# Sliding-window attention: 20 projection units in place of 24, and a new order of dense and attention work

## The reference, cut to what matters

```python
def swa_sink_mixer(h, cos, sin, w_in, sinks, w_out):
    q, k, v, gate = jnp.split(
        h @ w_in, [ATT_WIDTH, ATT_WIDTH + ATT_KV_WIDTH, ATT_WIDTH + 2 * ATT_KV_WIDTH], axis=-1)
    q = apply_partial_rope(q.reshape(b, L, ATT_Q_HEADS, D).astype(f32), cos, sin)
    k = apply_partial_rope(k.reshape(b, L, Hk, D).astype(f32), cos, sin)
    ...
    s = jnp.einsum('bnikgd,bnjkd->bnkgij', qb, kb) * (D ** -0.5)
    ...
    s = jnp.where(valid[None, :, None, None], s, -jnp.inf)
    sink = sinks.astype(f32).reshape(Hk, ATT_GQA)[None, None, :, :, None, None]
    m = jnp.maximum(jnp.max(s, axis=-1, keepdims=True), sink)
    p = jnp.exp(s - m)
    denom = jnp.sum(p, axis=-1, keepdims=True) + jnp.exp(sink - m)
    o = jnp.einsum('bnkgij,bnjkd->bnikgd', p / denom, vb)
    o = o.reshape(b, L, ATT_WIDTH) * jax.nn.silu(gate.astype(f32))
    return o.astype(h.dtype) @ w_out
```

## Time and profile before

| | |
|---|---|
| median of 3 runs | 2375.59 us (2370.33 to 2377.56) |
| the profiled execution: its own time | 2370.34 us |
| its span | 2368.2 us |
| PE busy | 2182.2 us, 92% |
| VectorE busy | 1474.7 us, 62% |
| ScalarE busy | 1020.0 us, 43% |
| SWA from its first rotations to its last P·V | 541.46 to 753.36 us |

### The profile page before, as it was taken

How to read it: one execution, slowest core, us unless ns; L and a number is a source line. 1 busy time by engine, 2 the same in 40 slices (tenths; PEclk the granted TensorE clock), 3 DMA queues, 4 the chain that set the end, 5 groups by cost and what they waited for, 6 DMA issues and landing times. The chain is left out here.

```text
span 2368.2 us, 41250 instructions
## 1 busy us (share of the span) xinstructions
PE 2182.2 (92%) x15127; PEld 1923.1 (81%) x15127; DVE 1474.7 (62%) x3067; ACT 1020.0 (43%) x1896; POOL 47.8 (2%) x37
## 2 busy tenths in 40 slices
PE   5999996989996899997999999989899889999998
PEld 4777775866674688886999999977777679999997
DVE  6778776446654567775566663259666655666522
ACT  4565554334444345554444442233455444344312
POOL 1000000000000000000000000022200000000000
PEclk7999997989997899998999999988999879999998
DMA  4533322243200211111333332411111113333330
GB/s 122 144 103 97 102 66 58 85 84 81 63 27 18 71 45 54 53 45 36 90 89 89 89 108 87 89 54 36 51 36 35 45 54 90 89 96 89 107 96 37
DMA packets 361350, 172.37 MB, mean 73 GB/s; under 512 B 67647, under 2 KB 359336, under 8 KB 361256
## 3 DMA queue, kind: packets, MB, share of 16 engines
q1 hardware_dynamic: 360616, 170.28, 26.3%
q0 software_dynamic: 640, 0.87, 0.3%
HBM read 168.68 MB, written 2.16 MB: 72 GB/s over the span
## 5 line engine op out<-in xcount | busy, mean ns | idle before, releaser
L278 PE MATMUL ps<-h_parts,parts 128*128 128x264 f32 (+3 forms) x8672 | 1335.5, 313 | 38.0 <-DVE h_parts L645 16.3
L278 PEld LDWEIGHTS ps<-h_parts,parts 128*128 128x128 f32 x8672 | 1195.8, 191 | 138.1 <-issue 43.1
L237 ACT ACTIVATE parts<-ring 128x1024 fp32r<-128x1024 f32 (+1 forms) x286 | 311.1, 1092 | 726.1 <-PE ps L278 494.6
L253 DVE TENSOR_TENSOR parts<-ring,parts 128x1024 fp32r<-128x1024 f32 (+1 forms) x270 | 341.5, 1269 | 209.8 <-ACT parts L237 208.8
L278 PE MATMUL ps<-wide_parts,parts 128*128 128x264 f32 (+3 forms) x1152 | 350.2, 304 | 0.0
L278 PE MATMUL ps<-up_hidden,parts 128*128 128x264 f32 (+1 forms) x1408 | 253.7, 283 | 1.7 <-PEq L2331 1.7
L278 PEld LDWEIGHTS ps<-wide_parts,parts 128*128 128x128 f32 x1152 | 220.6, 191 | 8.9
L278 PEld LDWEIGHTS ps<-up_hidden,parts 128*128 128x128 f32 x1408 | 216.9, 188 | 2.1 <-issue 2.1
L2314 DVE TENSOR_TENSOR up_u<-ps,norm_rstd 128x264 f32<-128x264 f32 (+2 forms) x176 | 74.7, 425 | 160.5 <-PE ps L278 153.1
L2584 DVE TENSOR_TENSOR res<-ps,res 128x264 f32<-128x264 f32 (+2 forms) x64 | 27.1, 428 | 101.1 <-PE ps L278 94.7
L278 PE MATMUL ps<-gated_high,parts 128*128 128x512 f32 x256 | 81.7, 400 | 3.4 <-DVE wide_parts L1202 3.4
(11 more groups left out here) (308 smaller groups left out, 2414.1 us busy)
## 6 DMA issues: line engine op xcount, KB each, us to landing
ring<-in_ffn_w_up SPq DMA_DIRECT2D x88, 512.0 KB, 3.8
ring<-in_ssm_w_in SPq DMA_DIRECT2D x48, 512.0 KB, 4.1
ring<-in_ffn_w_down SPq DMA_DIRECT2D x32, 704.0 KB, 4.6
ring<-in_att_w_in SPq DMA_DIRECT2D x48, 256.0 KB, 3.6
ring<-in_da_w_qkv SPq DMA_DIRECT2D x24, 512.0 KB, 3.8
ring<-in_dsa_w_in SPq DMA_DIRECT2D x24, 512.0 KB, 3.8
ssm_prefix<-prefix_rows SPq DMA_DIRECT2D x32, 256.0 KB, 4.0
ring<-in_ssm_w_out SPq DMA_DIRECT2D x16, 512.0 KB, 4.0
```

The costliest lines, as they stand in the source:

```text
L237: self.nc.scalar.activation(self.part(st, u, 0), self.slot(u, st.kt), ACT.Copy).then_inc(self.w_high, 1)
L253: self.nc.vector.tensor_tensor(self.part(st, u, 1), self.slot(u, st.kt), self.part(st, u, 0).bitcast(F32), ALU.subtract).then_inc(self.w_l ...
L278: m = self.nc.tensor.matmul(out, w[:, n], b, start=start and f == j == 0, stop=stop and f == st.kt - 1 and j == 2)
```

## The change

- K and V units hold the heads of two groups (2a and 2a+1), 64 columns each; a query unit pairs a head of group 2a with one of group 2a+1. There are 2 + 2 + 8 + 8 = 20 units. A step works on four query heads, two of each group of the pair; K and V are made once for two steps.
- The units form one list, `SWA_UNITS`, in the order of PE. The stream has one iteration of 20 units over 6 slots of the ring.
- A step's units (those from its gates to the ones ahead of the next gates) are cut: two whole units for slots 0 and 1, and the rest in four equal pieces for slots 2 to 5: 18, 18, 12 matmuls in steps 0 to 2. Step 3 has two units and cuts them 15 and 9, then 6, 6, 6, 6.
- On PE scores stand ahead of a slot's dense piece and transposes behind it, a slot later than before. P·V 2 and 3 and transposes 3 of a step stand in slots 0 and 1 of the next. V's transposes are made in steps 0 and 2 alone. Rotations use banks 2 and 3.
- On ScalarE silu stands behind the exps of blocks 0 and 1, in the last step the second at the end. On VectorE the output multiplies stand behind the next step's rope; the low parts of units are taken after the gates and after some of the blocks.
- The output is held in another order of heads, so a unit of output weights is loaded by four transfers in place of one, of 64 partitions each (`heads=True`).
- PE's steps are no loop any more.

PE in the softmax slots of step 0, before: P·V of block 0, transposes of block 1, scores of block 2, and so on to the step's end. L1425 is scores, L1434 transposes, L1445 P·V, L278 dense matmuls.

The diff, cut to its core:

```diff
+SWA_UNITS = [(x[0], int(x[1])) for x in "k0 v0 q0 q1 g0 g1 q2 q3 k1 g2 g3 v1 q4 q5 g4 g5 q6 q7 g6 g7".split()]
...
+        slot = self.slot(x, st.kt).rearrange("p (k n) -> p k n", k=st.kt)
...
-            sp.dma_start(slot[:, :, c0:c0 + n], cols(w, r0, st.kt, c, n)).then_inc(self.loaded[u], 16)
+            if st.heads:
+                for a in range(2):
+                    for b in range(2):
+                        rows = w[512 * a + 256 * b:512 * a + 256 * b + 256, bass.ds(c, n)]
+                        sp.dma_start(slot[64 * b:64 * b + 64, 4 * a:4 * a + 4, c0:c0 + n],
+                                     rows.rearrange("(r d) n -> d r n", d=64)).then_inc(self.loaded[x], 16)
+            else:
...
+    def items(s):
+        return [("k", s // 2)] * (s % 2 == 0) + [("q", 2 * s), ("q", 2 * s + 1)]
...
+    gates_at = [at["g", 2 * s] for s in range(KV)] + [len(SWA_UNITS)]
...
+    def slots(s):
+        mine = [(n, f) for n in range(gates_at[s], gates_at[s + 1]) for f in T8]
+        rest = len(mine) - 2 * KT
+        sizes = [KT, KT] + [rest // 4] * 4 if rest else [5, 3, 2, 2, 2, 2]
+        res = []
+        for z in sizes:
+            part, mine = mine[:z], mine[z:]
+            res.append([(n, [f for m, f in part if m == n]) for n in sorted({m for m, _ in part})])
+        return res
...
-                def piece(i, q):
-                    k.split_ready(pe, st, i, q)
-                    wait(pe, sem["lin_free"], 6 * i + q - 1)
-                    k.product(st, q, ps[:, q % 2, :], k.hx(0, SEQ)).then_inc(sem["lin_done"], 1)
-                def rot(s, q):
-                    pe.wait_ge(sem["lin_free"], 6 * s + order[q] + 1)
-                    if q == 0:
-                        wait(pe, sem["pt"], 4 * s)
-                    if q == 2:
-                        pe.wait_ge(sem["rope"], 3 * s + 1)
-                    nc.tensor.matmul(ps[:, 4 + q % 2, :], k.rot1, raw[:, q, :], start=True, stop=True).then_inc(sem["rot"], 1)
+                def linear(chunk):
+                    for n, tiles in chunk:
+                        if tiles[0] == 0:
+                            k.split_ready(pe, st, 0, n)
+                            wait(pe, sem["lin_free"], n - 1)
+                        m = k.product(st, n, bank(n), k.hx(0, SEQ), tiles=tiles)
+                        if tiles[-1] == KT - 1:
+                            m.then_inc(sem["lin_done"], 1)
+                def rot(s, j):
+                    x = items(s)[j]
+                    pe.wait_ge(sem["lin_free"], at[x] + 1 if s or j else 3)
+                    if j == 0:
+                        wait(pe, sem["masked"], 16 * s)
+                    if j == 2:
+                        pe.wait_ge(sem["rope"], ropes[s] + 1)
+                    nc.tensor.matmul(ps[:, 2 + j % 2, :], k.rot1, raw[:, place(x), :], start=True, stop=True).then_inc(sem["rot"], 1)
...
                 def vtr(s):
-                    pe.wait_ge(sem["lin_free"], 6 * s + 2)
-                    wait(pe, sem["masked"], 16 * s)
+                    pe.wait_ge(sem["lin_free"], at["v", s // 2] + 1)
...
                     for t in range(4):
-                        m = nc.tensor.transpose(ps[:, 2, t * P:(t + 1) * P], vT[:, t * P:(t + 1) * P], k.ident)
...
                     m.then_inc(sem["vtr"], 1)
...
-                def step(s, last=False):
-                    for q in range(6):
+                def step(s):
+                    for q, chunk in enumerate(slots(s)):
                         if q == 0:
                             rot(s, 0), rot(s, 1)
-                        if q == 1:
+                            if s:
+                                pv(s - 1, 2)
+                        if q == 1 and s % 2 == 0:
                             rot(s, 2)
-                            if isinstance(s, int) and s == 0:
+                            if s == 0:
                                 pre.pe_tokens(pe)
                             vtr(s)
-                        if q == 2:
-                            scores(s, 0)
-                        if q == 3:
-                            trans(s, 0), scores(s, 1)
-                        if q == 4:
-                            pv(s, 0), trans(s, 1), scores(s, 2)
-                        if q == 5:
-                            pv(s, 1), trans(s, 2), scores(s, 3)
-                        if q < 2:
-                            piece(s, 4 + q)
-                        elif not last:
-                            piece(s + 1, q - 2)
-                    pv(s, 2), trans(s, 3), pv(s, 3)
+                        if q >= 2:
+                            scores(s, q - 2)
+                        if q >= 4:
+                            pv(s, q - 4)
+                        linear(chunk)
+                        if q == 0 and s:
+                            trans(s - 1, 3)
+                        if q == 1 and s:
+                            pv(s - 1, 3)
+                        if q >= 3:
+                            trans(s, q - 3)
                 pre.pe(pe, st, [(u, 0, SEQ, u) for u in range(3)], sem["lin_done"])
-                piece(0, 3)
+                linear([(3, T8)])
                 pre.pe_sum(pe)
-                step(0)
...
+                def silu(s, j):
+                    act.wait_ge(sem["lin_free"], at["g", 2 * s + j] + 1)
+                    nc.scalar.activation(gate_tile(s, j), gate_tile(s, j), ACT.Silu).then_inc(sem["silu"], 1)
...
                 def step(s):
...
+                    last = s == KV - 1
+                    for q, chunk in enumerate(slots(s)):
+                        ends = [(n, sum(len(t) for m, t in chunk if m <= n)) for n, tiles in chunk if tiles[-1] == KT - 1]
+                        if q == 1 and s:
+                            store_pt(s - 1, 3)
+                        if q == 1 and s % 2 == 0:
                             if s == 0:
                                 pre.act_tokens(act, rtok)
                             vtok(s)
-                            exps(s, 0)
+                        for n, size in ends:
+                            if size <= 4:
+                                evict(n)
+                        if q >= 2:
+                            exps(s, q - 2)
+                        for n, size in ends:
+                            if size > 4:
+                                evict(n)
+                        if q == 2:
+                            silu(s, 0)
+                        if q == 3 and not last:
+                            silu(s, 1)
                         if q >= 3:
                             store_pt(s, q - 3)
-                            exps(s, q - 2)
-                        if q < 2:
-                            evict(s, 4 + q)
-                        elif s < KV - 1:
-                            evict(s + 1, q - 2)
-                    store_pt(s, 3)
...
+                silu(KV - 1, 1)
+                store_pt(KV - 1, 3)
...
+                def rope(s, j):
+                    x = items(s)[j]
...
+                    dve.wait_ge(sem["rot"], ropes[s] + j + 1)
...
+                    if place(x) == 0 or s % 2 and j == 0 or not s % 2 and j == 1:
+                        wait(dve, sem["s"], 4 * s)
+                    v.tensor_tensor(rop[:, place(x), :], t1[:], t2[:], ALU.add).then_inc(sem["rope"], 1)
+                    dve.wait_ge(sem["rope"], ropes[s] + j + 1)
...
+                def out(s):
                     dve.wait_ge(sem["pv"], 4 * s + 4)
...
+                def step(s):
+                    last = s == KV - 1
...
+                    for j in range(len(items(s))):
+                        rope(s, j)
+                        g = j - len(items(s)) + 2
+                        if g >= 0 and not (last and g):
+                            take_gate(s, g)
+                    if s:
+                        out(s - 1)
+                    more = list(range(gates_at[s] + 2, gates_at[s + 1]))
+                    for n in range(4):
+                        softmax(s, n)
+                        if n >= 4 - len(more):
+                            k.low_on_vector(dve, st, st.after(0, more[n - 4 + len(more)], st.depth))
+                    if last:
+                        take_gate(s, 1)
+                        out(s)
...
-            two = (u == 0, u == 1)
-            if two[0] or two[1]:
-                return twice(w_att, 1024 + 256 * u + 64 * j)
-            c = (256 * j, 128 + 256 * j, 1536 + 256 * j, 1664 + 256 * j)[u - 2]
-            return [(0, 64, w_att, 0, c), (64, 64, w_att, 0, c + 64)]
+        def swa_unit(i, n):
+            kind, x = SWA_UNITS[n]
+            if kind in "kv":
+                c, step = 1024 + 256 * "kv".index(kind) + P * x, 64
+            else:
+                c, step = 1536 * "qg".index(kind) + 512 * (x // 4) + 64 * (x % 4), 256
+            return [(0, 64, w_att, 0, c), (64, 64, w_att, 0, c + step)]
...
-            "swa": Stream(KV, 6, KT, swa_unit, dmas=2),
-            "swa_out": split(a["att_w_out"][0], KT),
```

(8 more changed lines are left out.)

182 lines of the change are left out of this document (94 added, 88 removed).

## The result

The changed kernel takes **2346.7 us** (median of 4 runs, 2345.5 to 2347.4) where the kernel before took 2376.5 beside it. The ratio is 0.9884 with a 95% interval of 0.9869 to 0.9899, so it is faster by 1.2%, some 27.6 us. A later repeat gave 2346.8 and 0.9887 (0.9870 to 0.9904).

What follows compares the result with a forecast made beforehand. TensorE, busy 92% of the span, was taken to bound the kernel. Stage −25.4 us and clock −2 gave −27.4, so 2342.9 from the profiled 2370.34, or 2348 us from the median, 5.2 higher; range 2337 to 2360.

Steps and rivals of the forecast that it cites:

- Dense work: Sliding-window attention on PE: four fewer units save 22.8 us, fewer rotations and V transposes 2.4 us.
- The wait for V: PE's 2.56 us wait before a step's first scores, for ScalarE's copies of V, was to disappear.
- New waits before P·V: PE waiting for ScalarE's copy of P: 3.1 and 2.7 us in step 1, 5.9 us before step 2's first P·V.
- The last step: Step 3's PE waits were to be 11.6 us: 1.5 moved P·V, 2.0 rope, 8 over its blocks.
- All waits together: PE's waits over the stage's four steps were to sum to 30.5 us, about the 28.8 of before.
- The clock: PE at 1.2 GHz in the stage was to cost 8 us, between 3 and 15, 2 less than before.
- the rival of more 1.2 GHz: More of the stage at 1.2 GHz, costing 15 us with waits as walked: −20.6, 2355 us; 24 in 100.
- The drain: Rival: a drain of about 1.38 us behind each ScalarE table load lengthens P·V chains; about −19, 2356 us; 3 in 100.
- Cover: Rival: dense work was only cover, softmax and copies bind the slots; −6, 2370 us; 6 in 100.
- The clock lost for good: Rival: PE falls to 1.2 GHz at step 0's first P·V and stays; slower, up to 2414 us; 2 in 100.
- Loads: Output projection weights by four transfers a unit, 24 more issues on SP's idle queue, costed at nothing.
- the 3 allowed: Sign of being wrong: the stages behind the changed one change by more than 3 us.

Runs made afterwards that it cites:

- e7: The changed kernel with output weights loaded by one transfer a unit, as before the change; 2347.2 us, ratio 0.9886.
- e9: The changed kernel with matmuls of no use filling PE's waits before P·V of blocks 0 and 1 (in step 2 only block 0); 2339.1 us, ratio 0.9867.
- e6: The changed kernel with a plain copy in place of each silu, so that the 15 table loads go; 2328.2 us, ratio 0.9812.
- e2: The kernel before, in its old order, with K and V units of the last three steps cut to half their contraction (72 matmuls fewer); 2361.0 us, ratio 0.9955.
- e1: The changed kernel with the 96 removed dense matmuls put back into slots 3 and 4 of steps 0 and 1; 2350.6 us, ratio 0.9910.
- e3: The changed kernel with both silus of steps 0 to 2 side by side ahead of block 0's exps; 2329.6 us, ratio 0.9821.
- e4: The changed kernel with P·V of blocks 0 and 1 behind their slot's dense piece on PE; 2329.6 us, ratio 0.9820.

## Why the prediction was right

The forecast was 2348 us, the measured median 2346.7. The mechanism came as walked, the closeness of the number is partly luck. The stage fell by 26.4 us where 27.4 were forecast. Between the two profiled executions the time fell by 23.0 us only, to 2347.4 where the same sum gave 2342.9, and by the ratio it fell by 27.6. Point by point:

- **Dense work.** 22.8 us and 2.4 us of work were to go; 25.5 went. The walk's own sum took more away, 201.7 − 28.8 − 145.8 = 27.1, 1.6 too much, and it had the waits 1.8 us too long. The 25.4 us for the stage at 2.4 GHz, against 25.6 measured, are so exact because these two errors cancel.
- **The wait for V** went, as walked. A wait of 0.15 us in step 0 is another one, for the rope ahead of V's transposes.
- **New waits before P·V.** Walked 3.1 and 2.7 us, measured 3.35 and 2.79 in both steps; step 2 walked 5.9, measured 6.13. The load by load walk along ScalarE's queue named the right instructions: the changed kernel has 15 loads, 8 before silus and 7 before exps.
- **The last step** was walked at 11.6 us of waits and has 10.0: 1.15 for the moved P·V (1.5 walked), 1.96 for rope (2.0) and 6.9 over its blocks (8). Before the change, PE stood 3.12 us ahead of the last transposes, not 3.6 to 3.7; the prediction's 14.2 us for that step holds. All waits together: 30.5 forecast, 28.7 measured, 28.8 before. "The idle time moves, it doesn't go" held to 0.1 us.
- **The clock** is the term that was mis-sized, by little: 9.9 of excess in place of 8, by the same count 10.7 before. The forecast took 2 us off it and 0.8 went. That it stayed nearly constant is the sum of two moves that the forecast didn't separate: in steps 0 to 2 it rose from 3.2 to 5.9 us, in the last step it fell from 7.5 to 4.0. The 8 was a guess between bounds: which of two equal waits is followed by a slow batch differs, as steps 0 and 1 show with the same 3.35 us, and e7 the other way round. e9 shows the cause; where it strikes stays open.
- **Against the rival of more 1.2 GHz** the text said that step 1 had such a wait and no slow unit. In the changed kernel step 1 has the largest excess of all, 4.2 us; in e7 it has none. The argument was weak; an excess of 9.9 lies between the forecast's 8 and the rival's 15.
- **The drain** doesn't show in the timeline, and e6's idle time has no room for it. **Cover**: e2 shows that this rival describes the old order in part, a third of a removal given back. The new order doesn't avoid it: by e1, 12.4 us of the 22.5 taken away came back as idle time, before P·V in place of the transposes. It takes the further moves of e3 or e4 to avoid that. **The clock lost for good** did not occur: after each wait PE was back at 2.4 GHz within the next batches.
- **Loads** were costed at nothing, and e7 confirms it. The stages behind the change differ by 2.1 us, inside the 3 allowed; the same stretch differs by up to 8 us between other kernels, so this sign tells little.

What the prediction did not draw from its own walk: it priced the silus between the exps at 3 us a step of PE's waits and went on. The same walk, done once more with the silus together or P·V a piece later, gives the 13 us that e3 and e4 found.

## What to carry to other kernels

When work is taken from the busiest engine, walk its queue again with the shorter pieces: each piece was also the cover of somebody's chain, and an order that asks for a result one piece later keeps the gain. Between two uses of one activation table put nothing that needs another: here seven more loads of 1.28 us put PE to waiting. Grouping them again (e3) brought 17 us, and so did asking for P·V one piece later with all loads in place (e4). Read a total against an account of work, idle time and excess at the low clock before giving it to a mechanism; by its total e6 could have been read as a second cost behind each load, which its account doesn't show.

## What was not expected of the hardware

A PE wait of 3 us can cost more than 3 us: of the batches behind a wait of 3.35 us one took 6.54 us and another 4.44, the granted clock being 0.90 and 1.00 in their steps. In every experiment that removed waits the excess fell with them, from 9.9 to between 1.6 and 6.6 us, and filling waits with useless matmuls made the stage 8.0 us shorter. The stretch behind the stage, the same instructions in all kernels with the changed load, took between 1612.8 and 1620.9 us in single profiled executions; a difference of a few microseconds between two totals says nothing until the stage itself is seen to differ.
